# Layer 1's memory gate made and stored turned, softmax evened before its transposes, and another order of the shared projections, in a two-layer hybrid decoder step

## The reference, cut to what matters

```python
def mem_attend(q, mem_kv):                      # 4 heads of 128, 256 memory rows
    s = einsum('bthe,bmhe->bhtm', q, mem_kv[:, :, 0])
    p = softmax(s, axis=-1)
    return einsum('bhtm,bmhe->bthe', p, mem_kv[:, :, 1])

def shared_kv(x, kv_norm_g, w_kv, k_norm_g):    # 3 groups: a key block (normed) and a value block each
    kv = (rms_norm(x, kv_norm_g) @ w_kv).reshape(b, t, 3, 2, 4, 128)
    return rms_norm(kv[:, :, :, 0], k_norm_g[:, None, :]), kv[:, :, :, 1]

def dil_layer(x, dil_fn, mem_kv, norm_g, w_in, q_norm_g, mem_q_g, w_out):
    z = rms_norm(x, norm_g) @ w_in
    qd, gd, mq, mg = split(z)                   # 3 x 512 queries, 512 gate, 512 query, 512 gate
    qd = rms_norm(qd) * 128 ** -0.5             # per head
    dil_out = dil_fn(qd) * silu(gd)
    q = rms_norm(mq) * 128 ** -0.5
    mem_out = mem_attend(q, mem_kv) * silu(mg)
    return x + concatenate([dil_out, mem_out], -1) @ w_out
```

## Time and profile before

| | us |
|---|---|
| median of 3 runs | 2721.64 |
| lowest, highest | 2720.32, 2723.96 |
| profiled execution | 2719.55 |
| its span | 2717.4 |
| PE busy in the span | 2702.2 |
| DVE, ACT, POOL busy | 1789.1, 1112.9, 383.1 |

### The profile page before, as it was taken

One profiled execution on the slowest core, in us unless ns is written; L12 is line 12 of the kernel. 1 busy time (PEld: TensorE's weight loads), 2 busy tenths in 40 slices (PEclk: granted clock), 3 DMA queues, 4 the chain that ended last, 5 costly groups with the idle time before them and its releaser, 6 DMA issues.

```text
span 2717.4 us, 41295 instructions
## 1 busy us (share of the span) xinstructions
PE 2702.2 (99%) x14834; PEld 2259.7 (83%) x14834; DVE 1789.1 (66%) x3925; ACT 1112.9 (41%) x3346; POOL 383.1 (14%) x610
## 2 busy tenths in 40 slices
PE   9999999999999999999999999999999999999999
PEld 7788888888887888878888888888888889998887
DVE  7686766768678644435575667877674767777764
ACT  7533131212326234225434353532332349876632
POOL 0101010100101000000112032333424223210000
PEclk9999999999999999999999999999999999999999
DMA  8486555655676734324266676787768789757642
GB/s 281 143 250 208 183 167 179 207 182 171 210 246 207 222 115 156 101 97 152 94 246 228 211 268 216 274 284 264 247 237 284 262 311 330 231 177 262 217 154 82
DMA packets 292628, 567.75 MB, mean 209 GB/s; under 512 B 32432, under 2 KB 91760, under 8 KB 292424
## 3 DMA queue, kind: packets, MB, share of 16 engines
q1 hardware_dynamic: 257032, 462.31, 52.0%
q0 software_dynamic: 35392, 102.80, 10.6%
HBM read 432.28 MB, written 132.72 MB: 208 GB/s over the span
## 4 chain that ended last, share of the span: by engine, by line
PE 93%; DVE 4%; DMA 1%; ACT 1%; issue 1%; SPq 0%; DVEq 0%; ACTq 0%
PE ps L130 27%; PE ps L132 26%; PE ps L131 26%; PE ps L4133 2%; PE ps L3736 2%; PE ps L1385 1%; PE ps L4142 1%; PE ps L3774 1%; PE ps L3719 1%; PE ps L3035 1%; PE ps L3040 1%; PE ps L228 1%; PE ps L3130 1%; DMA a_raws<-w_mem_dram 0%; DVE a_wp L124 0%
## 5 line engine op out<-in xcount | busy, mean ns | idle before, releaser
L130 PE MATMUL ps<-b_wp,b_sring 128*128 128x512 f32 x640 | 250.5, 391 | 0.0
L131 PE MATMUL ps<-b_wp,b_sring 128*128 128x512 f32 x640 | 249.2, 389 | 0.0
L132 PE MATMUL ps<-b_wp,b_sring 128*128 128x512 f32 x640 | 249.1, 389 | 0.0
L130 PE MATMUL ps<-a_sring,a_wp 128*128 128x512 f32 x512 | 200.0, 391 | 0.0
L131 PE MATMUL ps<-a_sring,a_wp 128*128 128x512 f32 x512 | 199.3, 389 | 0.0
L132 PE MATMUL ps<-a_sring,a_wp 128*128 128x512 f32 x512 | 199.2, 389 | 0.0
L130 PE MATMUL ps<-b_wp,b_xthi 128*128 128x512 f32 x480 | 188.3, 392 | 0.0
L131 PE MATMUL ps<-b_wp,b_xthi 128*128 128x512 f32 x480 | 187.0, 389 | 0.0
L132 PE MATMUL ps<-b_wp,b_xtlo 128*128 128x512 f32 x480 | 186.7, 389 | 0.0
L1200 DVE TENSOR_TENSOR shared_o<-ps,b_spare 128x512 f32<-128x512 f32 x160 | 109.7, 685 | 112.3 <-PE ps L132 97.1
L1032 ACT ACTIVATE ps<-shared_o 128x128 f32<-128x128 f32 x390 | 103.4, 265 | 163.2 <-DVE shared_o L1200 146.0
(11 more groups left out here) (494 smaller groups left out, 6877.3 us busy)
## 6 DMA issues: line engine op xcount, KB each, us to landing
b_sring<-sums_dram SPq DMA_DIRECT2D x160, 512.0 KB, 5.2
a_sring<-sums_a_dram SPq DMA_DIRECT2D x128, 512.0 KB, 5.1
b_raws<-w_b_dram SPq DMA_DIRECT2D x176, 256.0 KB, 4.5
a_raws<-w_a_dram SPq DMA_DIRECT2D x140, 256.0 KB, 4.1
kv_dram<-shared_o POOLq DMA_DIRECT2D x96, 256.0 KB, 4.0
tok_b_dram<-shared_o POOLq DMA_DIRECT2D x96, 256.0 KB, 4.3
front<-tok_b_dram SPq DMA_DIRECT2D x96, 256.0 KB, 3.9
front<-grp_dram SPq DMA_DIRECT2D x48, 260.0 KB, 4.2
```

The source lines that it names most:

```text
L130: pe.matmul(acc, a_hi, b_hi, start=first, stop=False)
L131: pe.matmul(acc, a_hi, b_lo, start=False, stop=False)
L132: return pe.matmul(acc, a_lo, b_hi, start=False, stop=last)
```

## The change

Five things are done together.

1. In shared_stage the opening makes the memory query block and gate(5) instead of key(0) and value(0). Gate(5) is made with the weights as stationary operand, so that it comes out turned, and goes to a new array `gate_b_t`. Its finishing in the opening is a sigmoid on ACT and then a multiplication on DVE, where it was one copy on ACT.
2. The pairs change: the second is now query(2) with gate(4), the last is value(0) with key(0), where it was gate(4) with gate(5). The last pair's f = 5 and 6 are thus of kind "norm", which was "silu", and f = 1 and 4 of kind "copy".
3. out_stage of layer 1 does as layer 0 did: it evens the probabilities before they are turned, its values product comes out turned, and the gate is one multiplication. `turn_o` is gone. `turn_mix` stands ahead of `turn_probs`, joint maximum, group weights and weighted sum of tile t+1 stand at the end of step t, and the joining's multiplications are split in two parts around maxima.
4. Decode.project takes the rows whole: four fp32 matmuls (8 stationary columns, 128 moving columns, one for each head's columns, written to different groups of 32 partitions) where one of 512 columns stood. The low copies go, and project(1) waits for all additions of half 0 (`y_added`).
5. At the end of dil_stage the first gate tiles are loaded turned, and its last DVE copy waits for the shared stage's outputs.

```diff
 shared_stage, opening:
-                        if i == 0:
-                            act.wait_ge(o_done, SAMPLES)
-                        act.activation(row, product, ACT.Copy).then_inc(o_done, 1)
+                        act.activation(row, product, ACT.Sigmoid).then_inc(acted, 1)
...
+                        dve.wait_ge(acted, acted_at[out] + 1)
+                        row = view(o[:, out % RING, :], out)
+                        dve.tensor_tensor(row, view(ps[:, bank, :], out), row, ALU.mult).then_inc(o_done, 1)
...
+                        elif b:
+                            chans, tokens = turned_at(i)
+                            m = split3(pe, ps[:, out % 4, :], wh[b][:, k, chans], wl[b][:, k, chans],
+                                       xt_hi[:, k, tokens], xt_lo[:, k, tokens], k == 0, k == KD - 1)
 build:
-                pairs = [Pair(query(0), query(1), norm_b, 2),
-                         Pair(query(2), Block("norm", io["tok_b"][3], 7, w_of(9)), norm_b, 2),
+                first = (Block("norm", io["tok_b"][3], 7, w_of(9)), gate(5))
+                pairs = [Pair(query(0), query(1), norm_b, 2), Pair(query(2), gate(4), norm_b, 2),
                          Pair(key(1), value(1), kv_norm, 1), Pair(key(2), value(2), kv_norm, 1),
-                         Pair(gate(4), gate(5), norm_b, 2)]
+                         Pair(value(0), key(0), kv_norm, 1)]
 Decode:
-            pe.wait_ge(self.y_begun, 1)
+            pe.wait_ge(self.y_added, 1)
...
-            acc = self.bank(slice(0, LOW + S), slice(0, C))
-            pe.matmul(acc, self.cat[:, k, :], w_hi, start=(k == 0), stop=False)
-            m = pe.matmul(acc, self.cat[:, k, :], w_lo, start=False, stop=(k == self.KO - 1))
+            for part, w in enumerate(self.operands.wo(k, half)):
+                for h in range(H):
+                    m = pe.matmul(self.projected_at(h), self.cat[:, k, 0:S], w.bitcast(F32)[:, h * HD:(h + 1) * HD],
+                                  start=(k == 0 and part == 0), stop=(k == self.KO - 1 and part == 1))
...
-        dve.tensor_tensor(xs, self.bank(slice(0, S), slice(0, C)), xs, ALU.add).then_inc(self.y_begun, 1)
-        dve.wait_ge(self.y_begun, half + 1)
-        dve.tensor_tensor(xs, self.low, xs, ALU.add).then_inc(self.y_added, 1)
+        for h in range(H):
+            xs = self.xs[:, half, h * HD:(h + 1) * HD]
+            m = dve.tensor_tensor(xs, self.projected_at(h), xs, ALU.add)
+        m.then_inc(self.y_added, 1)
 out_stage, ACT:
-                exponentials(t, (0, 1))
-                if not conv and t > 1:
-                    weighted_sum(t)
-                exponentials(t, (2, 3)).then_inc(exped, 1)
+                exponentials(t, range(H)).then_inc(exped, 1)
...
                     mix_high(t)
+                    if t + 1 < NT:
+                        group_weights(t + 1)
+                        weighted_sum(t + 1)
 out_stage, DVE:
             def invert(t):
                 dve.wait_ge(exped, t + 1)
                 dve.reciprocal(stat[:, 3, :], stat[:, 2, :]).then_inc(inverted, 1)
-                if conv:
-                    dve.wait_ge(inverted, t + 1)
-                    for h in range(H):
-                        m = dve.tensor_scalar(prob[:, h, :], prob[:, h, :], stat[:, 3, h:h + 1], None, ALU.mult)
-                    m.then_inc(evened, 1)
+                even(t)
 out_stage, PE:
             def turn_probs(t):
-                pe.wait_ge(evened if conv else exped, t + 1)
+                pe.wait_ge(evened, t + 1)
...
                 else:
                     pe.wait_ge(mlo_done, 1)
                     project(0, 0, range(MIX))
+                    pe.wait_ge(front.o_left, 1)
+                    project(0, 1, range(1))
                 turn_probs(0)
...
                 scores(t)
-                if not conv:
-                    turn_o(t - 1)
                 left(t - 1)
                 dec_middle(t)
-                turn_probs(t)
                 if not conv:
                     turn_mix(t)
+                turn_probs(t)
 dil_stage, DVE:
                 if s == 0:
                     dve.wait_ge(first_done, 1)
+                    dve.wait_ge(*tail.outputs)
```

More of the change, by code:

```diff
@@ L696, in __init__, with shared_stage @@
         self.wh1, self.wl1 = prep.buffers(stack)
-def shared_stage(core, block, stack, lead, prep, first, pairs, ops, bufs, xt_hi, xt_lo, xs, zero, spare, w_out, keys, opening):
+def shared_stage(core, block, stack, lead, prep, first, turned_dst, pairs, ops, bufs, xt_hi, xt_lo, xs, zero, spare, w_out, keys, opening):
     nc, ps, io = core.nc, core.ps, core.io
@@ L721, in shared_stage @@
     outs = []
-    for blk in first:
-        for i in range(SAMPLES):
-            outs.append((blk.kind, P if i < NT else S, blk.dst[i * P:i * P + (P if i < NT else S), :], 0))
+    rows_block, turned_block = first
+    for i in range(SAMPLES):
+        n = P if i < NT else S
+        outs.append((rows_block.kind, n, rows_block.dst[i * P:i * P + n, :], 0))
+    turned_at = lambda i: (slice(i % H * P, (i % H + 1) * P), slice(i // H * C, (i // H + 1) * C))
+    for i in range(NT):
+        outs.append((turned_block.kind, P, turned_dst[turned_at(i)], 0))
+    outs.append((turned_block.kind, S, turned_block.dst[T:TS, :], 0))
     for pair in pairs:
@@ L3663, in step @@
                     low_o(0)
-                if not conv and t > 1:
-                    weights(t)
                 if conv or t > 1:
@@ L3735, in values @@
                         p, of = pt[:, h * MT + mt, :], v[:, mt, h, :]
-                        m = pe.matmul(sums[:, h, :], of if conv else p, p if conv else of, start=(mt == 0),
+                        m = pe.matmul(sums[:, h, :], of, p, start=(mt == 0),
                                       stop=(mt == MT - 1))
@@ L3830, in first @@
                 else:
-                    pe.wait_ge(front.o_left, 1)
-                    project(0, 1, range(MIX // 2))
+                    project(0, 1, range(1, MIX // 2))
                 dec_end(0)
```

146 lines of the change are left out of this document (52 added, 94 removed).

## The result

The changed kernel takes 2727.97 us (median of 12 runs, 2725.22 to 2730.35), the kernel before 2722.55 us in the runs beside it (2720.32 to 2723.96). The ratio is 1.0020, with a 95% interval of 1.0012 to 1.0028: slower by 5.4 us, where 7.5 us less were forecast. It lies outside the range, whose upper end was 2721.

The account below looks back on a forecast made before the run. PE was taken to bound the kernel, busy 2702.2 of 2717.4 us. Terms -9.4 - 6.6 + 1.5 + 1.75 + 0.4 + 4.8 = -7.55 from 2719.55, plus 2.1 to the median, gave 2714.2 us; range 2709 to 2721.

Parts of the forecast that it names:

- The sample projection: Sample output projection, both layers: groups of four fp32 matmuls at 0.113 us run side by side, saving 9.4 us.
- Rival 3: Sample projection doesn't get shorter, since fp32 takes four passes: +1.9 us in the sum, 2723.5 us; chance 0.06.
- turn_o and the steps of layer 1: Layer 1's out_stage: transposes gone, 15 x 0.44 = -6.6 us; evening of probabilities hidden behind `left`, costing 0.
- Rival 2: Layer 1's steps: evening delays turn_probs in 14 steps; excess of 0.5 us each gives 2721; chance 0.20.
- The wait ahead of project(1): Layer 1's out_stage: project(1) waits for all additions of half 0, +1.5 us, bounds 1.0 and 2.2.
- The start of layer 1: Start of layer 1's out_stage: first turn_probs, first `left` and second turn_probs wait, +1.75 us, bounds 0.8 and 2.6.
- The opening: Opening of shared_stage: DVE's recombining ends later, first pair's weights and sums arrive just in time; +0.4 us.
- The transition: From shared_stage to dil_stage: norm tiles finishing later delay key copies and first scores; +4.8 us, bounds 3 and 7.
- The second pair: Pairs of shared_stage other than the last: change of place among equal kinds, none at a stage's edge, claimed costless.

## Why the prediction was wrong

**The sample projection: the step that failed.** The sum had -9.4 us, from a group of four at 0.113 us. It is 0.22, and the four projections together are 0.56 us shorter by their own rows, of which about 0.36 goes on a later start of 0.09 each: -0.2. The term was mis-sized: the step divided the time of the earlier trace rows by 32 groups, taking 128 records for 128 matmuls, where the code issues 64. The count could have been held against the code: 8 chunks, two parts, four heads. With 0.2 in place of 9.4 the sum would have been +1.6. Rival 3, with a chance of 0.06 and +1.9, was right in its place and mechanism, and its 2723.5 is 4.5 us short of the measured time, for the terms below.

**turn_o and the steps of layer 1: right.** -6.6 was forecast, and the wait for the evening to be hidden. The rows show 0.36 instead of 0.79 between scores and `left`, the evening ended at 5.4 us as worked out, tiles 3 to 14 gained 5.9 and the end some 1.0. Rival 2, the evening on the path, didn't happen: the kernel came out slower, but not by the only rival that stood on the slower side.

**The wait ahead of project(1): right.** +1.5 forecast; 1.96 us between starts instead of 0.23, and tile 15 +1.09, which holds a turn_o less: about +1.6. The earlier additions took 1.6 away. What makes the wait is mostly the group weights ahead of the additions, which the prediction named too: with the projection of before, and only the first addition asked for, 1.50 of the 1.96 stayed.

**The start of layer 1: right in size, half in place.** +1.75 forecast, 1.39 and 0.58 measured: +2.0. The first `left` waits for the low part, as named (0.80). The first wait, 0.65, isn't at turn_probs: the three matmuls put ahead of it wait for ACT's copy of the last dilated sums (`dil_o`), and the evening ends just as they do. The second turn_probs waits for nothing.

**The opening: about right.** +0.4 forecast, 0.15 measured.

**The transition: right in part, short in size.** +4.8 with an upper bound of 7 was forecast; the first sums came 7.0 us later by this stretch in one profile and 6.6 in the other, and 5.5 to 6.3 in the three without a fall of the clock. The first scores were to wait for the second key copy, and did, by 2.08 us, since the wait for slots grew: 2.85 us ahead of the fourth tile's addition, where the first pair had 1.72. What the sum didn't have is ACT's query copies behind squares and root: 3.12 of the 5.20 us of idle time wait for them. Nor did it have a clock that falls where PE waits, with some 1 us.

**The second pair: missed.** It was called costless, as a change of place among equal kinds. It wasn't: silu tiles came where norm tiles had been, +1.3 (the cause in part open, above).

With the measured terms (the steps of layer 1 and the end -6.8, tile 15 as it stands +1.1, the mean of the two profiles for the transition): -0.2 - 6.8 + 1.1 + 2.0 + 0.15 + 6.8 + 1.3 = +4.35, and 0.3 to 0.6 more at the end of dil_stage. The medians differ by 5.4 and 4.5. The chance of 0.58 for faster rested on the one term.

## What to carry to other kernels

Hold the count of records against the code before dividing a time by it: one instruction may leave two. A block's finishing belongs to its place: what is cheap in the middle of a stage (two key blocks in the third pair: 0.0 to 0.15 us) costs 4.5 to 7 us in the last pair, where other work stands behind it on the same engines (the next stage's first copies, the output weights). So the lightest blocks go last. Follow every engine that a finishing uses: here PE waited longer for ACT (3.12 us) than for DVE (2.08). And when a buffer or bank is given back by another engine or at another moment than before, look at what that engine has queued just there.

## What the runs showed of the hardware

An fp32 matmul of 8 stationary and 128 moving columns takes PE 0.22 us, alone or as one of four that write to different groups of 32 partitions, and leaves two records of 0.27 us for each. Four multiplications of 128x128 on DVE took 2.39 us while POOL multiplied 128x512 (1.31 us), against 1.14 without it. The length of stretches that wait for transfers varied by up to 2.6 us between executions of the same kernel, while the stretches of layer 1's out_stage agreed within 0.3.

PE's granted clock fell to 0.5 (1.2 GHz) for 3.41 us, ahead of the last few us of the span, in four of the eleven profiles of the changed kernel and its variants. Each time PE was in a wait of 2.08 to 2.49 us or had come out of one shortly before; in three other profiles it waited 1.7 to 2.5 us at the transition and the clock stayed at 1.0. Eight score matmuls took 3.08 us in one such stretch, against 1.78.
